# Twelve groups of matmuls take the columns of their moving operand in other orders

## The reference

```
proj = x @ w_in[l]                                   # 1024 -> 8200: q, k, v, gates ...
y_ret = (head_norm(retention(q, k, v)) * silu(r_g)) @ w_proj_ret[l]
y_ml  = (head_norm(mlstm(...)) * sigmoid(m_o)) @ w_proj_mlstm[l]
x = layer_norm(ALPHA * x + (gate_a * y_ret + gate_b * y_ml) @ w_out[l])
gu = x @ w_gate_up[l]                                # 1024 -> 2 * 2816
x = layer_norm(ALPHA * x + (silu(gu[..., :2816]) * gu[..., 2816:]) @ w_down[l])
```

## Time and profile before

| | |
|---|---|
| runs of the kernel | 1158.3 and 1158.4 us, median 1158.35 us |
| span of the profiled execution, first to last instruction | 1157.2 us |
| TensorE busy | 1144.6 us, 99% of the span |
| weight loads busy (they lie beside matmuls) | 1040.2 us |
| VectorE busy | 773.0 us, 67% |
| ScalarE busy | 577.4 us, 50% |
| mean granted TensorE clock | 0.999 of full |

### The profile page before, as it was taken

The page is one execution under the profiler, slowest core; times in us unless marked ns, Lnnn a source line. Parts: engine busy times, 40 slices in busy tenths (PEclk is TensorE's granted clock), DMA queues, the critical chain, the costliest instruction groups (busy, mean ns, idle before and its releaser), DMA issues.

```text
span 1157.2 us, 18537 instructions
## 1 busy us (share of the span) xinstructions
PE 1144.6 (99%) x7762; PEld 1040.2 (90%) x7762; DVE 773.0 (67%) x1056; ACT 577.4 (50%) x668; POOL 28.8 (2%) x36
## 2 busy tenths in 40 slices
PE   9999999999999999999999999999999999999997
PEld 7989998998999988899998898899988789978996
DVE  5797856667655546697774668755555766875676
ACT  6565455433544434555544534444443456745663
POOL 0000000001000000000000000000000100010000
PEclk9999999999999999999999999999999999999999
DMA  8764464556666463745455556765566364447320
GB/s 290 278 205 154 154 210 161 196 187 203 222 202 199 162 207 125 236 165 176 137 193 187 176 189 218 228 205 179 190 200 216 138 218 120 136 144 247 126 95 37
DMA packets 129954, 211.62 MB, mean 183 GB/s; under 512 B 6608, under 2 KB 52688, under 8 KB 129744
## 3 DMA queue, kind: packets, MB, share of 16 engines
q1 hardware_dynamic: 128128, 204.15, 53.0%
q0 software_dynamic: 1744, 6.29, 1.7%
HBM read 209.37 MB, written 1.05 MB: 182 GB/s over the span
## 4 chain that ended last, share of the span: by engine, by line
PE 89%; ACT 3%; DVE 3%; issue 2%; DMA 1%; SPq 1%; POOL 0%; POOLq 0%; DVEq 0%; ACTq 0%
PE ps L509 87%; DMA raw<-in_w_in 1%; ACT wh L995 1%; DVE wl L1426 1%; PE ps L736 1%; PE ps L642 1%; PE ps L836 0%; ACT L1034 0%; SPq L445 0%; POOL small L464 0%; ACT L1037 0%; DVE xl L1520 0%; ACT ee L1313 0%; PE ps L818 0%; DVE zz L1990 0%
## 5 line engine op out<-in xcount | busy, mean ns | idle before, releaser
L1426 DVE TENSOR_TENSOR wl<-raw,wh 128x2048 fp32r<-128x2048 f32 (+1 forms) x186 | 415.1, 2237 | 168.4 <-ACT wh L995 168.1
L995 ACT ACTIVATE wh<-raw 128x2048 fp32r<-128x2048 f32 (+1 forms) x190 | 358.7, 1892 | 185.5 <-PE ps L509 161.8
L509 PE MATMUL ps<-xh,wh 128*128 128x256 f32 x1328 | 370.4, 279 | 1.5 <-issue 1.5
L509 PE MATMUL ps<-xl,wh 128*128 128x256 f32 x1328 | 367.2, 277 | 0.0
L509 PE MATMUL ps<-xh,wl 128*128 128x256 f32 x1312 | 363.4, 277 | 0.0
L509 PEld LDWEIGHTS ps<-xh,wh 128*128 128x128 f32 x1328 | 249.7, 188 | 4.7 <-issue 4.0
L509 PEld LDWEIGHTS ps<-xl,wh 128*128 128x128 f32 x1328 | 249.9, 188 | 0.2
L509 PEld LDWEIGHTS ps<-xh,wl 128*128 128x128 f32 x1312 | 246.7, 188 | 0.0
L509 PE MATMUL ps<-wh,xh 128*128 128x512 f32 (+1 forms) x440 | 171.9, 391 | 2.6 <-DVE xl L1520 1.6
L509 PE MATMUL ps<-wh,xl 128*128 128x512 f32 (+1 forms) x440 | 168.5, 383 | 0.0
L509 PE MATMUL ps<-wl,xh 128*128 128x512 f32 (+1 forms) x440 | 168.3, 382 | 0.0
(11 more groups left out here) (303 smaller groups left out, 1473.3 us busy)
## 6 DMA issues: line engine op xcount, KB each, us to landing
raw<-in_w_in SPq DMA_DIRECT2D x89, 1024.0 KB, 5.0
raw<-in_w_gate_up SPq DMA_DIRECT2D x88, 512.0 KB, 4.9
raw<-in_w_down SPq DMA_DIRECT2D x20, 1024.0 KB, 5.0
raw<-in_w_out SPq DMA_DIRECT2D x16, 1024.0 KB, 5.0
raw<-in_w_proj_ret SPq DMA_DIRECT2D x8, 1024.0 KB, 5.0
raw<-in_w_proj_mlstm SPq DMA_DIRECT2D x8, 1024.0 KB, 4.9
rows<-in_ln_g POOLq DMA_DIRECT2D x4, 512.0 KB, 4.3
rows<-in_ln_b POOLq DMA_DIRECT2D x4, 512.0 KB, 5.8
```

The lines of the kernel that those rows point to most:

```text
L509: return pe.matmul(o, a, b, start=start, stop=False, skip_group_check=True)
L995: act.activation(stretch(wh, u, 0, m), source(u)[:, 0:m], ACT.Copy).then_inc(s_hi, 1)
L1426: dve.tensor_tensor(stretch(wl, u, a, nk * n), source(u)[:, a:nk * n], f32(stretch(wh, u, a, nk * n)), ALU.subtract).then_inc(s_lo, 1 if a ...
```

## The change

Twelve groups of each layer of the first block take their columns in another order. A new function ordered rearranges three views with the same rule: the output, and the high and the low moving operand. Column i of the result thus still lands in its own place; only the order within an instruction differs. (j a e -> a j e) with a = 2 goes through every second piece of e elements and then through the others. (a j e -> j a e) with a = 2 goes back and forth between the two halves of the columns, e elements at a time. ff3, ff4, ff5, ff9, rg0 are of the first kind, ff6, ff7, ff8, ff10, rg1, mo0, mo1 of the second; pieces have 4, 16 or 32 elements, that is 16, 64 or 128 bytes. For ff9 and ff10 a is 4. The stationary operand stays as it is.

```diff
+ORDERS = {"ff3": ("p (j a e) -> p a j e", 2, 16), "ff4": ("p (j a e) -> p a j e", 2, 4), "ff5": ("p (j a e) -> p a j e", 2, 32),
+          "ff6": ("p (a j e) -> p j a e", 2, 16), "ff7": ("p (a j e) -> p j a e", 2, 32), "ff8": ("p (a j e) -> p j a e", 2, 4),
+          "ff9": ("p (j a e) -> p a j e", 4, 16), "ff10": ("p (a j e) -> p j a e", 4, 16),
+          "rg0": ("p (j a e) -> p a j e", 2, 16), "rg1": ("p (a j e) -> p j a e", 2, 16), "mo0": ("p (a j e) -> p j a e", 2, 32),
+          "mo1": ("p (a j e) -> p j a e", 2, 4)}
...
-            def tok3(o, lh, ll, k, t, h_, l_, start):
+            def ordered(name, v):
+                if name not in ORDERS:
+                    return v
+                how, a, e = ORDERS[name]
+                return v.rearrange(how, a=a, e=e)
+
+            def tok3(o, lh, ll, k, t, h_, l_, start, name=""):
+                o, h_, l_ = (ordered(name, v) for v in (o, h_, l_))
                 mm(o, lh[:, k, tok_half(t)], h_, start)
                 mm(o, lh[:, k, tok_half(t)], l_, False)
                 return mm(o, ll[:, k, tok_half(t)], h_, False)
...
-            def col3(o, lh, ll, k, h_, l_, start):
-                mm(o, h_, lh[:, k, :], start)
-                mm(o, h_, ll[:, k, :], False)
-                return mm(o, l_, lh[:, k, :], False)
+            def col3(o, lh, ll, k, h_, l_, start, name=""):
+                o, xh_, xl_ = (ordered(name, v) for v in (o, lh[:, k, :], ll[:, k, :]))
+                mm(o, h_, xh_, start)
+                mm(o, h_, xl_, False)
+                return mm(o, l_, xh_, False)
```

More of the change, by code:

```diff
@@ L576, in group @@
                             for t in range(2):
-                                r = tok3(banks[t][:, :], lh, ll, k, t, h_[:, kk, :], l_[:, kk, :], k == 0)
+                                r = tok3(banks[t][:, :], lh, ll, k, t, h_[:, kk, :], l_[:, kk, :], k == 0, name)
                         else:
@@ L580, in group @@
                                 o = banks[j // 2][:, S * (j % 2):S * (j % 2) + S]
-                                r = col3(o, lh, ll, k, h_[:, kk, tok_half(j)], l_[:, kk, tok_half(j)], k == 0 and j % 2 == 0)
+                                r = col3(o, lh, ll, k, h_[:, kk, tok_half(j)], l_[:, kk, tok_half(j)], k == 0 and j % 2 == 0, name)
                         k += 1
```

## The result

The changed kernel takes 1174.57 us (1174.49 and 1174.65), the kernel before 1158.35: a ratio of 1.0142 with a 95% interval of 1.0126 to 1.0158. It is 16.2 us slower.

What follows compares the result with a forecast made beforehand. TensorE's back-to-back matmul pace was taken as the bound. Short pieces 9.0 us plus load 2.6 us made 11.6 us, taking the span from 1157.2 to 1168.8 and the time to 1170 us; range 1156 to 1200.

Steps and rivals of the forecast that it cites:

- forecast case: Whole kernel: short pieces and load cost 11.6 us, giving 1170 us, within about 1161 to 1178; chance 0.43.
- (a): Moving stream in 64- and 128-byte pieces (ff3, ff5, ff6, ff7, ff9, ff10, rg0, rg1, mo0): 0 extra.
- (b): 16-byte pieces in ff4, ff8, mo1: extra cycles for more visits to 64-byte stretches, 9.0 us, bounds 0 and 11.5.
- (c): Stationary load meeting the reordered stream in twelve 256-column groups: 2.25 ns a matmul, 2.6 us, bounds 0 and 7.7.
- the phase: Load and stream in 256-column groups avoid each other at 113.3 ns; easily lost, as in rq at 117.8 ns.
- (d): PSUM output written in the same new order: taken as 0, though no row showed its cost.
- (e): ScalarE and VectorE making the next weights: TensorE doesn't wait for them, yr0 effect some tenths at most, left out.
- no change: Rival: the extra cycle goes by columns and the locked phase survives any order; 1158.5 us, chance 0.27.
- the output: Rival: breaks in PSUM addresses slow all 24 groups; halving the rate would give 1419 us; chance 0.05.
- The jump rival: Every break of address costs a cycle in read or write, 25.0 us, 1186 us with the load term; chance 0.10.
- The short piece: Rival: ff4, ff8 and mo1 take twice their time (1224 us) or four times (1354 us); chance 0.10.
- The rival of a gain: The extra cycle comes from sequential reading and goes with it; 1146 us, the most to be gained; chance 0.05.

Runs made afterwards that it cites:

- e2_output: Changed kernel with only the output in the twelve new orders, moving operand read in sequence: 1157.91 us, ratio 0.9999 to the kernel before.
- e11_all_wide: Kernel before with all 512-column groups reordered, 32-byte pieces 128 bytes apart in each block's first layer, 16-byte pieces 64 apart in the second: 1159.95 us, ratio 1.0018.
- e12_chosen: Kernel before with only rv0, rv1, rg0, rg1, mo0, dn0, dn1, q, k, av reordered, 32-byte pieces 128 bytes apart: 1152.75 us, ratio 0.9951.

## Why the prediction was right, and where it was off

The time was forecast at 1170 with the forecast case ending at 1178, and is 1174.6. The reading of the bound held: nothing but TensorE's pace moved, and every nanosecond a matmul went straight into the time. The mechanism behind the sum held only in part, and that the sum came near is in part luck. By the steps:

(a) Pieces of 64 and 128 bytes, taken as free in the stream: wrong. They cost 8 to 13 ns in a matmul of 512 columns, where the load has time to spare. rg0, rg1 and mo0 are 0.60, 0.64 and 0.37 us longer, 3.2 us over both layers for the 0 of the sum.

(b) Pieces of 16 bytes: right in rank, too large in size. Forecast 120, 133 and 267 ns for ff4, ff8, mo1; measured 117.7, 126.8 and 252; 5.6 us (2 x (0.42 + 1.29 + 1.11)) for 9.0. The unit behind it was misread: 64 bytes in a circle would have been free by it, and cost 241.7 ns, and pieces of 16 bytes at a distance of 64 or 256 bytes would have cost the same, and took 223.5 and 278. The paces of 8-byte pieces fit a unit of 16 bytes, though not in every order.

(c) The load: 2.6 us forecast, with bounds of 0 and 7.7. The six groups named there cost 2 x (0.77 + 0.64 + 0.64 + 0.52 + 0.63 + 0.64) = 7.7 us, the upper bound. The size was off, and so was the cause, as far as is shown: with the loads held in one place most of it stays. It belongs to (a), the stream. What I said of the phase is nonetheless real, but it needs no reordered group: in sequence the pace is 113.3 or 117.8 ns with the same addresses, depending on what ran ahead. No untouched group lost it in the changed kernel: outside of the touched groups no stretch changed by more than 0.1 us, the start of the kernel aside.

(d) The output at 0: right, shown by e2_output.

(e) The other engines at 0: right. yr0 got 0.1 us shorter (12.28 for 12.38), within the tenths that were left out.

So 3.2 + 5.6 + 7.7 = 16.5 us stand against 0 + 9.0 + 2.6 = 11.6. The total was near because the term for short pieces, too large by 3.4, made up for part of the terms for long ones, too small by 8.3. That is luck and not a result of the model.

Of the rivals, no change and the output fell with e2_output and the result. The jump rival was 11 us too high (1186) and isn't right in kind either: a fee per break can't make (16,4,8) faster than the sequence. The short piece isn't wrong in idea: pieces of 8 bytes about double the time in four of five orders, but no group of the change was that short. The rival of a gain had part of the mechanism, that the extra 6.25% isn't paid in every order, and the wrong orders: none of the twelve gained, while (16,4,8) and (32,4,4) did in some groups.

## What to carry to other kernels

When a kernel is bound by back-to-back fp32r matmuls, read the pace from starts or from windows cut at groups, and compare it with columns over clock: the remainder is where order and placement act. By these runs moving operands may be broken into pieces of 256 bytes at no cost, and outputs as finely as 16 bytes; breaking the moving operand into pieces of 16 to 128 bytes costs 2 to 23% unless the order is one of the few good ones, and 8-byte pieces can double the time. Put different variants into different groups of one kernel and check them in both layers, but look at the untouched groups as well: what stands behind a reordered group can change its pace, and a local gain be lost there. For the same reason measure the combination that you want to keep: gains of single groups didn't add up here (5.4 us of 7.5).

## What was not expected of the hardware

- The sequence isn't the fastest way to read an fp32r moving operand. 512 columns take 226.7 ns in sequence, 220.0 in pieces of 32 bytes at a distance of 128 bytes, 223.5 in pieces of 16 at 64, and 216.5 when the same 16 bytes are read again and again.
- Reading the same 64 bytes again and again takes 241.7 ns for 512 columns, more than the sequence.
- Untouched groups held 117.8 ns over 768 matmuls in a row where they held 113.3 before, with all addresses the same.
- q, k and av of one layer, in the same order, took 35.27 us in one kernel and 36.27 in another that differs in the order of the groups' columns ahead of them.

What stays open: the arrangement of memory behind the table of paces. Lengths and distances were varied, but the addresses of the moving operand only by what the groups happen to use, and (16,4,8) at 220 in rg0 and dn0 but 228 and 231 in out0 and mv1 isn't explained. Pieces of 8 bytes were never given to one side alone. Whether the second pace of the col groups is a collision of load and stream was not shown either; that the sequence alone has two paces was. Which of the groups reordered in e11_all_wide, but not in e12_chosen, upset ff2 to ff10 was not tried one by one.
